# Feed-forward up products of a three-block fp32 network: two input parts in one 512-column matmul

## The reference, cut to what matters

```python
D_MODEL = 1024
SEQ = 256
D_FF = 2816

def _rmsnorm(x, g):
    x32 = x.astype(jnp.float32)
    y = x32 * lax.rsqrt(jnp.mean(x32 * x32, axis=-1, keepdims=True) + RMS_EPS)
    return (y * g.astype(jnp.float32)).astype(x.dtype)

def _swiglu(x, w_gate, w_up, w_down):
    return (jax.nn.silu(x @ w_gate) * (x @ w_up)) @ w_down

x = x + 0.5 * _swiglu(_rmsnorm(x, ffn1_norm[l]), ffn1_w_gate[l], ffn1_w_up[l], ffn1_w_down[l])
```

## Time and profile before

| what | value |
|---|---|
| median of three runs | 4002.84 us (4000.92 to 4006.6) |
| profiled execution, span on its page | 4004.4 us |
| TensorE matmuls (PE) | 98% of the span, 34150 instructions |
| TensorE weight loads (PEld) | 95%, 34150 |
| VectorE (DVE) | 68%, 4071 |
| ScalarE (ACT) | 50%, 2620 |
| GpSimd (POOL) | 5%, 277 |
| share of the chain that ended last | PE 87%, DVE 7%, ACT 4% |
| 16 DMA engines, on average | 180 GB/s |

### The profile page before, as it was taken

One profiled execution on the slowest core, in us unless ns is written; L12 is line 12 of the kernel. 1 busy time (PEld: TensorE's weight loads), 2 busy tenths in 40 slices (PEclk: granted clock), 3 DMA queues, 4 the chain that ended last, 5 costly groups with the idle time before them and its releaser, 6 DMA issues.

```text
span 4004.4 us, 78708 instructions
## 1 busy us (share of the span) xinstructions
PE 3909.7 (98%) x34150; PEld 3793.3 (95%) x34150; DVE 2736.3 (68%) x4071; ACT 1987.8 (50%) x2620; POOL 212.2 (5%) x277
## 2 busy tenths in 40 slices
PE   8999999999999999999999999999999999999999
PEld 8979999889998999999997999999998899999999
DVE  6566665666655656567555799956756699974855
ACT  5445444454544545465435545754444544764443
POOL 0011000110002000010023000000000000000000
PEclk9999999999999999999998999999999999999999
DMA  6534555345555455534550455456654455455754
GB/s 237 192 115 151 192 190 190 133 148 195 181 194 182 160 199 184 195 133 173 191 204 34 159 194 181 177 199 233 229 196 153 158 177 193 175 182 202 265 199 158
DMA packets 114791, 720.78 MB, mean 180 GB/s; under 512 B 13328, under 2 KB 13664, under 8 KB 32784
## 3 DMA queue, kind: packets, MB, share of 16 engines
q1 hardware_dynamic: 90144, 652.25, 45.9%
q10 hardware_dynamic: 19200, 37.01, 2.5%
q0 software_dynamic: 5104, 26.49, 1.9%
HBM read 692.48 MB, written 23.22 MB: 179 GB/s over the span
## 4 chain that ended last, share of the span: by engine, by line
PE 87%; DVE 7%; ACT 4%; issue 1%; POOL 0%; DMA 0%; ACTq 0%; DVEq 0%; POOLq 0%
PE psum L655 26%; PE psum L657 26%; PE psum L656 26%; PE psum L1408 3%; DVE slab_low L1916 2%; ACT slab_high L1427 2%; DVE h_parts L2219 1%; PE psum L1065 1%; PE psum L1048 1%; PE psum L875 1%; PE psum L1078 1%; ACT room L1670 1%; DVE room L2248 0%; DVE room L2253 0%; PE psum L1349 0%
## 5 line engine op out<-in xcount | busy, mean ns | idle before, releaser
L1916 DVE TENSOR_TENSOR slab_low<-slab,slab_high 128x2048 fp32r<-128x2048 f32 x622 | 1423.2, 2289 | 738.8 <-ACT slab_high L1427 736.6
L655 PE MATMUL psum<-h_parts,slab_high 128*128 128x256 f32 x5632 | 1578.2, 280 | 28.9 <-DVE h_parts L2219 18.6
L1427 ACT ACTIVATE slab_high<-slab 128x2048 fp32r<-128x2048 f32 x622 | 1189.3, 1912 | 785.4 <-PE psum L657 721.1
L656 PE MATMUL psum<-h_parts,slab_high 128*128 128x256 f32 x5632 | 1556.5, 276 | 0.0
L657 PE MATMUL psum<-h_parts,slab_low 128*128 128x256 f32 x5632 | 1556.1, 276 | 0.0
L655 PEld LDWEIGHTS psum<-h_parts,slab_high 128*128 128x128 f32 x5632 | 1063.5, 189 | 48.8 <-issue 24.0
L655 PE MATMUL psum<-hidden_parts,slab_high 128*128 128x256 f32 x3840 | 1063.5, 277 | 11.4 <-DVE hidden_parts L2166 4.8
L656 PEld LDWEIGHTS psum<-h_parts,slab_high 128*128 128x128 f32 x5632 | 1063.5, 189 | 2.4 <-issue 2.2
L657 PEld LDWEIGHTS psum<-h_parts,slab_low 128*128 128x128 f32 x5632 | 1062.8, 189 | 0.0
L656 PE MATMUL psum<-hidden_parts,slab_high 128*128 128x256 f32 x3840 | 1058.0, 276 | 0.0
L657 PE MATMUL psum<-hidden_parts,slab_low 128*128 128x256 f32 x3840 | 1058.0, 276 | 0.0
(11 more groups left out here) (346 smaller groups left out, 3326.0 us busy)
## 6 DMA issues: line engine op xcount, KB each, us to landing
slab<-in_up SPq DMA_DIRECT2D x176, 1024.0 KB, 4.8
slab<-in_keys_up SPq DMA_DIRECT2D x128, 1024.0 KB, 4.8
slab<-in_keys_down SPq DMA_DIRECT2D x128, 1024.0 KB, 4.8
slab<-in_down SPq DMA_DIRECT2D x88, 1024.0 KB, 4.8
slab<-in_w_in SPq DMA_DIRECT2D x16, 1024.0 KB, 4.8
slab<-in_wq SPq DMA_DIRECT2D x16, 1024.0 KB, 4.8
peer_gates<-room ACTq DMA_DIRECT2D x64, 256.0 KB, 2.3
room<-peer_gates ACTq DMA_DIRECT2D x64, 256.0 KB, 5.4
```

Of the source, the lines that this page charges most:

```text
L655: nc.tensor.matmul(out, lhs[0], rhs[0], start=first, stop=False, **options)
L656: nc.tensor.matmul(out, lhs[0], rhs[1], start=False, stop=False, **options)
L1427: nc.scalar.activation(k.high[m % PARTS][:, 0:width], k.slabs[m % RING][:, 0:width], ACT.Copy).then_inc(k.rounded.up())
L1916: nc.vector.tensor_tensor(k.low[m % RING][:, 0:width], k.slabs[m % RING][:, 0:width], k.high[m % PARTS][:, 0:width], ALU.subtract).then_in ...
```

## The change

A new helper `wide_product` makes a product of two matmuls: the high weights by both input parts at once, 512 columns into a whole bank, and the low weights by the high input, 256 columns into its first half. The second half then holds high weights by low input. ScalarE copies both banks' second halves to a new SBUF tile `seconds` (L1526 of the changed file) one tick after the matmuls. VectorE adds them to the first halves (L2033, signal `up_summed`, which now frees the bank pair), and multiplies by 1/rms in a second operation (L2035, `up_scaled`). All that follows for the same f comes one tick later than before, and both loops have one tick more. The down products and all other stages keep `product`.

```diff
+    def wide_product(self, bank, lhs, rhs, first, last):
+
+        nc = self.k.nc
+        both = bank.rearrange("p (a t) -> p a t", a=2)
+        if last:
+            nc.tensor.matmul(bank[:, 0:T], lhs[1], rhs[:, 0, :], start=False, stop=False)
+            return nc.tensor.matmul(both, lhs[0], rhs, start=False, stop=True)
+        nc.tensor.matmul(both, lhs[0], rhs, start=first, stop=False)
+        return nc.tensor.matmul(bank[:, 0:T], lhs[1], rhs[:, 0, :], start=False, stop=False)
...
             if f >= 4:
-                nc.tensor.wait_ge(k.up_scaled.sem, k.up_scaled.at(f - 3))
+                nc.tensor.wait_ge(k.up_summed.sem, k.up_summed.at(f - 3))
...
-                        mm = self.product(pair[:, a], [part[:, a, c, :] for part in w], (k.h[:, c, 0, :], k.h[:, c, 1, :]), c == 0, c == DC - 1)
+                        mm = self.wide_product(pair[:, a], [part[:, a, c, :] for part in w], k.h[:, c], c == 0, c == DC - 1)
...
                     if f == 0 and n % 2 == 0:
-                        nc.tensor.wait_ge(k.up_scaled.sem, k.up_scaled.at(FC - 3 + n // 2))
+                        nc.tensor.wait_ge(k.up_summed.sem, k.up_summed.at(FC - 3 + n // 2))
...
-            if 1 <= tick <= FC:
-                f = tick - 1
+            if 2 <= tick < FC + 2:
+                f = tick - 2
                 gate = v.both[:, f % 2, 0]
                 nc.scalar.wait_ge(k.up_scaled.sem, k.up_scaled.at(f + 1))
                 nc.scalar.activation(gate, gate, ACT.Silu).then_inc(k.gated.up())
+            if 1 <= tick <= FC:
+                f = tick - 1
+                nc.scalar.wait_ge(k.slab_done.sem, k.slab_done.at(f + 1))
+                if f >= 2:
+                    nc.scalar.wait_ge(k.up_summed.sem, k.up_summed.at(f - 1))
+                nc.scalar.activation(v.seconds[:, f % 2], k.bank_pairs[(f + k.first_pair) % 4][:, :, T:2 * T], ACT.Copy).then_inc(k.second_copied.up())
...
-            if tick < FC:
-                f = tick
+            if 1 <= tick <= FC:
+                f = tick - 1
                 both = v.both[:, f % 2]
-                nc.vector.wait_ge(k.slab_done.sem, k.slab_done.at(f + 1))
+                nc.vector.wait_ge(k.second_copied.sem, k.second_copied.at(f + 1))
                 if f >= 2:
                     nc.vector.wait_ge(k.multiplied.sem, k.multiplied.at(f - 1))
-                nc.vector.tensor_tensor(both, k.bank_pairs[(f + k.first_pair) % 4][:, :, 0:T], v.rstd.unsqueeze(1).to_broadcast([P, 2, T]),
-                                        ALU.mult).then_inc(k.up_scaled.up())
+                pair = k.bank_pairs[(f + k.first_pair) % 4]
+                nc.vector.tensor_tensor(both, pair[:, :, 0:T], v.seconds[:, f % 2], ALU.add).then_inc(k.up_summed.up())
+                nc.vector.wait_ge(k.up_summed.sem, k.up_summed.at(f + 1))
+                nc.vector.tensor_tensor(both, both, v.rstd.unsqueeze(1).to_broadcast([P, 2, T]), ALU.mult).then_inc(k.up_scaled.up())
```

More of the change, by code:

```diff
@@ L229, in __init__ @@
         self.dve_step, self.act_step, self.pool_step, self.pe_step = (signal(f"{e}_step") for e in ("dve", "act", "pool", "pe"))
-        self.up_scaled, self.gated, self.multiplied = signal("up_scaled"), signal("gated"), signal("multiplied")
+        self.up_summed, self.up_scaled, self.gated, self.multiplied = (signal(n) for n in ("up_summed", "up_scaled", "gated", "multiplied"))
+        self.second_copied = signal("second_copied")
         self.pair_done = signal("pair_done")
@@ L352, in ffn_views @@
     v.square, v.squares, v.rstd = k.carve(DC, T), k.carve(2, T), k.carve(T)
-    v.both, v.acts = k.carve(2, 2, T), k.carve(2, T)
+    v.both, v.seconds, v.acts = k.carve(2, 2, T), k.carve(2, 2, T), k.carve(2, T)
     if fold:
@@ L691, in ffn @@
             at = (f + k.first_pair) % 4
-            pair = k.bank_pairs[at][:, :, 0:T]
+            pair = k.bank_pairs[at]
             if f >= 4:
-                nc.tensor.wait_ge(k.up_scaled.sem, k.up_scaled.at(f - 3))
+                nc.tensor.wait_ge(k.up_summed.sem, k.up_summed.at(f - 3))
             elif f >= 2 or k.first_pair < 2:
@@ L703, in ffn @@
                 firsts, lag = [], FIRST_LAG if first else DC if k.before == "ffn" else 2
-                pairs = [k.bank_pairs[g + k.first_pair][:, :, 0:T] for g in range(2)]
+                pairs = [k.bank_pairs[g + k.first_pair] for g in range(2)]
                 for step in range(DC + lag):
@@ L714, in ffn @@
                         for a in range(2):
-                            mm = self.product(pairs[g][:, a], [part[:, a, c, :] for part in firsts[g]], (k.h[:, c, 0, :], k.h[:, c, 1, :]), c == 0, c == DC - 1)
+                            mm = self.wide_product(pairs[g][:, a], [part[:, a, c, :] for part in firsts[g]], k.h[:, c], c == 0, c == DC - 1)
                         if c == DC - 1:
@@ L733, in ffn @@
             if f == 5 and first:
-                nc.tensor.wait_ge(k.up_scaled.sem, k.up_scaled.at(4))
+                nc.tensor.wait_ge(k.up_summed.sem, k.up_summed.at(4))
                 self.bias_lines()
@@ L1489, in ffn @@
                     square.then_inc(k.squared.up())
-        for tick in range(FC + 2):
+        for tick in range(FC + 3):
             if (2 if fold else 0) <= tick < FC:
@@ L1500, in ffn @@
                 nc.scalar.dma_start(k.bias_views.table[0:32, :], k.dram["bias_table"]).then_inc(k.small.up(), 16)
-            if tick >= 2:
-                f = tick - 2
+            if tick >= 3:
+                f = tick - 3
                 nc.scalar.wait_ge(k.multiplied.sem, k.multiplied.at(f + 1))
                 nc.scalar.activation(k.hidden[:, f, 0, :], v.acts[:, f % 2, :], ACT.Copy).then_inc(k.hidden_rounded.up())
-            if 1 <= tick <= FC:
-                f = tick - 1
+            if 2 <= tick < FC + 2:
+                f = tick - 2
                 gate = v.both[:, f % 2, 0]
```

## The result

The change makes the kernel slower. Over four runs each (one more of the kernel before than the three whose median was 4002.84 us), the median went from 4003.8 us (4000.92 to 4006.6) to 4037.88 us (4033.5 to 4039.87), a ratio of 1.0081 with a 95% interval of 1.0069 to 1.0094: 0.8% slower where 0.6% faster was forecast. The profiled execution has a span of 4034.7 us against 4004.4.

A forecast was written before the change was run, and what follows sets the result against it. The prediction took TensorE to bound the kernel, with weight load slightly longer than a 256-column stream. Its terms, -31.0 + 7.2 - 2.5 + 1.1 = -25.2 us, gave 3977.6 us against the runs' median, range 3961 to 3994.

The forecast's parts named there:

- What bounds the kernel: In the up slabs TensorE was taken as the bound, busy 106.30 of 106.50 us, with room on DVE and ACT.
- The matmuls: 2816 up products were to take 329 ns (216 wide, 113 narrow) instead of 340: -31.0 us.
- rival 3: In the up products, a wide matmul costs two narrow ones, 226.7 ns: about +5 us, 4008 us, chance 0.08.
- Rival 4: Wide up matmuls lose fp32r's full rate: 430 ns each, +572 us, 4575 us; chance 0.06 with smaller forms.
- the floor of 112 ns per load: Each matmul with new weights takes about 112 ns however few columns follow; claimed to set the 256-column matmul's 113.
- The rule that I set against the trace: N / 2.4 + 2.5 ns per matmul, 109 and 216; by it alone the change gains 7 us.
- The work beside it: Added DVE and ACT work during steady ups was to cost nothing, with 5 us of cover.
- The end of the ups: TensorE was to wait 0.9 us in each first down slab, before n = 6, eight times: +7.2 us.
- The starts: At the start of the ups in seven stages, the 0.36 us wait for slab 3 was to go: -2.5 us.
- The fold stage: Its 0.82 us wait for slab 4 goes, but gains until slab 6 are given back: +1.1 us.
- rival 2: In the up products, the weight load vanishes altogether: -36.5 us in all, 3966 us, chance 0.10.

## Why the prediction was wrong

**What bounds the kernel: right.** TensorE without idle time, DVE and ACT with room. DVE went from 71% to 80% of the stretch, ACT from 50% to 56%, and PE has no idle time in the steady ups.

**The matmuls: wrong, and with it the whole sum.** Two sentences failed. "I take 216, nearest to the 512-cycle records": even in step it is 226.7, the upper end that I had given and rival 3. "The 256-column one stays at 113": it went to 118.7, and the wide one above its upper end to 232.1. The term was to be -31.0. It is +31 by the steady banks, and +27 by whole stages (23.4 us, and the 4.1 that the starts gave back). That the two numbers have the same size is chance. Rival 3 named the right price in step, and the part missing from it, 11 ns per product, is the loss of step, which no rival had. Half of it is on the narrow one (5.4 ns), half on the wide one (5.4 ns over 226.7). Rival 4 had the sign but not the mechanism; the columns keep their rate, as 0.43 us at half clock shows.

The reading behind it was the floor of 112 ns per load. That floor exists, but it does not make the 113, since a wide matmul in step, with 213 ns of columns to cover the next load, pays twice the same addition: I took two numbers that lie close together for cause and effect. A row of the same trace spoke against it, and I had seen only its neighbours in the earlier trace rows. This is the timeline of PE before, in the stage behind the last feed-forward one, where plain fp32 matmuls are mixed in:

```profile
2034.63 0.28 PE L655 MATMUL psum<-h_parts,slab_high 128*128 128x256 f32 x1
2034.75 0.28 PE L656 MATMUL psum<-h_parts,slab_high 128*128 128x256 f32 x1
2034.87 0.28 PE L657 MATMUL psum<-h_parts,slab_low 128*128 128x256 f32 x1
2034.99 0.28 PE L655 MATMUL psum<-h_parts,slab_high 128*128 128x256 f32 x1
```

The same instruction with its own load, and 0.118 us. The matmuls behind the first one of the earlier trace rows show it as well, inside the ups:

```profile
364.08 0.28 PE L656 MATMUL psum<-h_parts,slab_high 128*128 128x256 f32 x1
...
365.26 0.28 PE L657 MATMUL psum<-h_parts,slab_low 128*128 128x256 f32 x1
```

Ten distances in 1.18 us, and then 113 to 114 again. A load floor gives one number everywhere. Two numbers for one instruction meant that 113 was a state to be kept.

The rule that I set against the trace, 2.5 ns per matmul beside its columns (the Trainium skill, TensorE: Matmul & The Clock Gate, "Back-to-back issue gap"; that section gives it for a matmul alone, and not for a stream with a weight load per matmul, which is what runs here), gave a gain of 7 us and is not borne out here either: 226.7 for 512 columns in step is 13 ns above them, 113.3 for 256 is 6.6.

**The work beside it: right.** It costs nothing but at the ends. The run with everything but the matmuls is at 1.0009 (0.9999 to 1.0019).

**The end of the ups: right in kind, smaller in size.** The pause is 0.56 us per stage instead of 0.9; with what follows it, 0.73, it comes to 5.8 us instead of 7.2. With slabs of 5.61 us instead of 5.26 the queues on DVE and ACT had more time; in the run with slabs of 5.44 the pause was 0.75 and the whole 0.90. A term is missing from the sum here and at the starts: behind a wait the first matmul stands 227 ns before the next, and nine more stand at 118 on average, together 0.16 us that the sum put at nothing.

**The starts: right, and worth more.** No wait for slab 3 is left. In the run with narrow matmuls, which has the up matmuls of the kernel before, slabs 2 and 3 of a stage (counted from 0) become shorter by 0.36 and 0.16 us, so 3.6 us in seven stages instead of 2.5. **The fold stage: half right.** Its wait of about 1 us went as forecast. The new one at slab 6 does not come in the change, whose slabs are slower than assumed; in the run with narrow matmuls it is there, 0.36 us.

One small slip in the sums: rival 2 by its own terms is -36.2 us, not -36.5. Nothing hangs on it.

Shown by runs: the loss is the matmuls' own (everything else alone costs 0.1%); a wide one never stands less than 224 ns before the next and in step costs what two narrow ones cost; one matmul of another length, or a wait, slows some ten equal narrow ones behind it; the distance in SBUF between weights and moving columns decides whether the narrow ones find a step. Open: what inside the chip makes the step, why it takes 10 to 13 narrow matmuls to come back, why equal wide ones mostly stay out of it, and why 6.6 ns per 256 columns remain in it. No run looked for a distance at which a mixture of lengths, or the wide ones alone, would lose nothing.

## What to carry to other kernels

Before a matmul stream is changed, compare the start distances of one and the same instruction all over the trace: if they have more than one value, the lower one is a state, and an edit that brings in a matmul of another length, a wait, or tiles at another place can lose it, for many matmuls at once. A matmul saved by making another one longer is worth only what the fixed part per matmul is, and that has to be measured with columns doubled, not read off short matmuls. It has to be read over the whole trace, too: four rows of the all-wide run say 227 ns, its 5632 wide matmuls say 230.5. And where a kernel places tiles at an odd offset, as with byte 240 here, that offset is part of its tuning: here it carries 3% of the time.

## What the runs showed of the hardware that I had not expected

- One fp32r matmul of 256 columns with new weights is 113.3 ns after the last in a steady run and 117 to 119 ns on average in an unsteady one, at a granted clock of 1.00 both times. At half clock it is 213 ns in the kernel before, and wide ones in the change are 427: the columns alone.
- Wide ones of 512 columns, all equal, have two lasting patterns at full clock: 226 to 227 ns, or 225, 231 and 237 or 238 in turn. One stretch of the second lasted for 640 matmuls.
- After two matmuls of 128 columns in such a run, 113 comes back behind the tenth matmul (1.24 us); after two wide ones, behind the thirteenth narrow one (1.55 us). After a wait (363.85 us in the kernel before) the first takes 227 ns, and 113 comes back behind the tenth.
- Moving the moving operand's tiles by 240 bytes, with the weights left in place, costs the kernel before 3.3% (3.0 to 3.6); moving weights and columns together by 128 bytes costs the changed kernel nothing that its interval shows.
